# Halved products in the first FFNs of a two-layer hybrid block, and the state space matrices made one third later

## The reference

```python
for l in range(DEPTH):
    x = x + 0.5 * swiglu(rms_norm(x, ffn1_norm[l]), ffn1_w1[l], ffn1_w3[l], ffn1_w2[l])
    h = rms_norm(x, mix_norm[l])
    p = h @ w_in[l]                       # inputs of four branches
    ...                                   # mamba2, s5 (state space), sparse attention, hgrn2
    x = x + merged @ w_out[l]
    x = x + 0.5 * swiglu(rms_norm(x, ffn2_norm[l]), ffn2_w1[l], ffn2_w3[l], ffn2_w2[l])

def swiglu(x, w1, w3, w2):                # w1, w3: 1024 x 2816, w2: 2816 x 1024
    return (jax.nn.silu(x @ w1) * (x @ w3)) @ w2
```

## Time and profile before

| what | value |
|---|---|
| median of 3 runs | 2779.82 us (2779.58 to 2780.38) |
| profiled execution | 2778.9 us, span 2777.1 us |
| granted TensorE clock | 1.00 in the mean |
| TensorE busy | 2771.6 us (100%) |
| its weight loads | 2332.3 us (84%) |
| VectorE, ScalarE, GpSimd busy | 1746.9 (63%), 1272.2 (46%), 845.8 us (30%) |
| DMA | 284.57 MB, mean 102 GB/s |
| chain that ended last | TensorE 98% |

### The profile page before, as it was taken

How to read it: one execution, slowest core, us unless ns; L and a number is a source line. 1 busy time by engine, 2 the same in 40 slices (tenths; PEclk the granted TensorE clock), 3 DMA queues, 4 the chain that set the end, 5 groups by cost and what they waited for, 6 DMA issues and landing times.

```text
span 2777.1 us, 41251 instructions
## 1 busy us (share of the span) xinstructions
PE 2771.6 (100%) x15610; PEld 2332.3 (84%) x15610; DVE 1746.9 (63%) x2736; ACT 1272.2 (46%) x1944; POOL 845.8 (30%) x412
## 2 busy tenths in 40 slices
PE   9999999999999999999999999999999999999999
PEld 8888888877788888898988888888777888898988
DVE  5585557685657447585744855576856674585755
ACT  5343344556355446353543423445553553453533
POOL 0075014333333442131100850233333343421321
PEclk9999999999999999999999999999999999999999
DMA  5323573222222232233333235732222222323323
GB/s 199 98 91 117 142 159 116 82 76 69 81 87 79 90 94 98 91 115 99 107 129 98 91 129 136 159 107 84 69 76 76 84 84 91 94 90 105 108 95 103
DMA packets 113091, 284.57 MB, mean 102 GB/s; under 512 B 35616, under 2 KB 45344, under 8 KB 112416
## 3 DMA queue, kind: packets, MB, share of 16 engines
q1 hardware_dynamic: 112928, 282.35, 32.8%
HBM read 268.67 MB, written 9.44 MB: 100 GB/s over the span
## 4 chain that ended last, share of the span: by engine, by line
PE 98%; DVE 1%; ACT 0%; issue 0%; DMA 0%; SPq 0%; ACTq 0%; DVEq 0%
PE bank L594 25%; PE bank L596 24%; PE bank L595 24%; PE bank L678 5%; PE bank L679 5%; PE bank L680 4%; PE bank L622 1%; PE bank L624 1%; PE bank L623 1%; PE bank L987 1%; PE bank L1006 1%; PE bank L1021 1%; PE bank L767 1%; PE bank L1120 1%; PE bank L961 0%; PE bank L974 0%
## 5 line engine op out<-in xcount | busy, mean ns | idle before, releaser
L464 POOL TENSOR_TENSOR w_lo<-raw,w_hi 128x1024 fp32r<-128x1024 f32 x208 | 519.5, 2502 | 1080.9 <-ACT w_hi L456 1080.9
L594 PE MATMUL bank<-h_hi,w_hi 128*128 128x512 f32 x1872 | 736.8, 394 | 0.6 <-DVE silu_a L2160 0.3
L596 PE MATMUL bank<-h_hi,w_lo 128*128 128x512 f32 x1872 | 729.1, 389 | 0.0
L595 PE MATMUL bank<-h_lo,w_hi 128*128 128x512 f32 x1872 | 728.9, 389 | 0.0
L456 ACT ACTIVATE w_hi<-raw 128x1024 fp32r<-128x1024 f32 x374 | 393.4, 1056 | 562.6 <-PE bank L596 537.4
L594 PEld LDWEIGHTS bank<-h_hi,w_hi 128*128 128x128 f32 x1872 | 351.4, 188 | 80.6 <-issue 7.1
L596 PEld LDWEIGHTS bank<-h_hi,w_lo 128*128 128x128 f32 x1872 | 351.4, 188 | 74.0
L595 PEld LDWEIGHTS bank<-h_lo,w_hi 128*128 128x128 f32 x1872 | 351.6, 188 | 70.7
L464 DVE TENSOR_TENSOR w_lo<-raw,w_hi 128x1024 fp32r<-128x1024 f32 x166 | 230.9, 1391 | 169.7 <-ACT w_hi L456 169.4
L514 POOL TENSOR_TENSOR w_lo<-raw,w_hi 128x1024 fp32r<-128x1024 f32 x76 | 139.3, 1853 | 445.4 <-DVE bank L2211 445.4
L594 PE MATMUL bank<-g_hi,w_hi 128*128 128x512 f32 x698 | 272.1, 390 | 0.2
(11 more groups left out here) (441 smaller groups left out, 5178.3 us busy)
## 6 DMA issues: line engine op xcount, KB each, us to landing
raw<-in_w_lots SPq DMA_DIRECT2D x478, 512.0 KB, 3.5
s_wd<-s_z SPq DMA_DIRECT2D x8, 512.0 KB, 3.5
s_t<-s_taps SPq DMA_DIRECT2D x16, 256.0 KB, 13.2
da_s<-da_qk SPq DMA_DIRECT2D x16, 256.0 KB, 3.9
x<-in_x SPq DMA_DIRECT2D x8, 256.0 KB, 6.0
raw_k<-in_w_lots SPq DMA_DIRECT2D x8, 256.0 KB, 6.3
s_w_re<-s_wd SPq DMA_DIRECT2D x32, 64.0 KB, 3.5
s_w_im<-s_wd SPq DMA_DIRECT2D x32, 64.0 KB, 3.4
```

What stands on the lines that cost most here:

```text
L464: eng.tensor_tensor(w_lo[:, s], raw[:, s], w_hi[:, s].bitcast(f32), SUB).then_inc(S["lo_done"], 1)
L594: pe.matmul(b[:, :], w_hi[:, s, kw], xh[:, k], start=(k == 0), stop=False)
L595: pe.matmul(b[:, :], w_hi[:, s, kw], xl[:, k], start=False, stop=False)
L596: return pe.matmul(b[:, :], w_lo[:, s, kw], xh[:, k], start=False, stop=(k == nk - 1))
```

## The change

- `PLAIN_PAIRS` now has an entry for each FFN of each layer: ffn1 of layer 0 has six plain pairs in its first third, none in the second and six (all) in the last; ffn1 of layer 1 has three, none and six; ffn2 stays as it was. So 2 + 8 = 10 and 5 + 8 = 13 pairs of ffn1 become halved.
- ffn1 uses the code of ffn2 for that (`halved`, `three_plain`), and new code for layer 0 (`six_plain`). ScalarE writes the unrounded h for it (`normed_of`, `hn_first`). The pairs' loops are written out; in the second third the early start of the first two down lots falls away.
- `s5_prepare` moves one third later: phases 0 and 1 at the second third's down lots, 2 behind the last third's pairs, 3 (VectorE) ahead of the last two pairs of the last third, 4 into the last third's down lots, ahead of the last one. TensorE makes the taps behind the sixth of these lots.
- GpSimd first does its share of ffn1's halved pairs, then `s5_matrices`, now with the input matrices (`s5_gen`) ahead of the output ones (`s5_ca_ready`).
- SP: the turned matrices are stored ahead of the third down lot of the last third, 24 of the 32 fetches stand ahead of the lots 64 to 71 (three per lot from lot 64 to 71), the other eight behind the taps' stores, and the lots 72 to 75 behind those.
- In the last tile of the stage before ffn2, `tile_of` makes `h_lo` ahead of the sum of squares.
- Some buffers move.

```diff
-PLAIN_PAIRS = (3, 0, 0)
+PLAIN_PAIRS = (((6, 0, 6), (3, 0, 6)), ((3, 0, 0), (3, 0, 0)))
...
+            def halved(n, i0, J):
+
+                first = n + 2 * i0
+                for a in range(first, n + 2 * J, 2):
+                    q1(a)
+                    if a > first:
+                        q3(a - 2)
+                    q5(a)
+                    q6(a)
+                    if a > first:
+                        q4(a - 2)
+                    q2(a)
+                    q7(a)
+                q3(n + 2 * J - 2)
+                q4(n + 2 * J - 2)
...
+                    if i0 < J:
+                        halved(n, i0, J)
+                    n, g0 = n + 2 * J, g0 + J
+                    if th < len(THIRDS) - 1:
+                        down(n, J, g0)
+                    else:
+                        for j in range(KT):
+                            gemm(n + j, 0, g_hi, g_lo, J, ready=("g_done", g0 - J) if j == 0 else None)
+                            if j == 5:
+                                s5_taps_of()
...
+                for n in range(4, MIX0 + 4):
+                    if n == 12 and layer == 0:
+                        sp.dma_start(con[:, upper:freq], con_in[:, upper:freq]).then_inc(S["c_rest"], 16)
+                    if n == FIRST_LOT[0][1] + 21:
+
+                        sp.wait_ge(S["out_done"], OUT[FIRST_LOT[0][1] + 15] + 1)
...
+                    if n == MIX0 - 6:
+                        for i in range(4):
+                            sp.wait_ge(S["s5_w_turned"], i + 1)
...
+                    if n >= MIX0 - 4:
+                        if n == MIX0 - 4:
+                            sp.wait_ge(S["s5_w_out"], 16 * 4)
+                        fetch_w(3 * (n - MIX0 + 4), 3 * (n - MIX0 + 5))
+                    lot_in(n)
                 sp.wait_ge(S["s5_tap_d"], 4)
                 taps = s5_taps.rearrange("i (j g) c -> g i j c", g=8)
                 for g in range(8):
                     sp.dma_start(taps[g], s5_tap[16 * g:16 * g + 16]).then_inc(S["s5_tap_out"], 16)
-                ring(MIX0 // 4, MIX0 // 4 + 2)
+                fetch_w(24, 32)
+                ring(MIX0 // 4 + 1, MIX0 // 4 + 2)
...
+                    else:
+                        s5_prepare(2)
+                        for j in range(KT):
+                            if j == KT - 1:
+                                s5_prepare(4)
+                            split_hi(act, n + j + 4)
+                            tile_of(1, j, (OUT[n + j], 0))
...
             def tile_of(r, i):
+                if r == 2 and i == KT - 1:
+                    low(r, i)
+                    add_square(r, i)
+                    return
                 add_square(r, i)
                 low(r, i)
...
+                    else:
+                        for j in range(KT):
+                            down(n, j, 0)
+                            split_lo(V, n + j + 4, 0)
+                            tile_of(1, j)
+                            if j == KT - 2:
+                                s5_prepare(4)
```

More of the change, by code:

```diff
@@ L729, in ffn2 @@
                         norm_sums(2)
-                        for j in range(2, 2 * PLAIN_PAIRS[0]):
+                        for j in range(2, 2 * i0):
                             gemm(n + j, 0, h_hi, h_lo, KT)
[L732 to L745, removed]
+                        pe.wait_ge(S["w0_in_t_lo"], s_at(1, S4))
+                    halved(n, i0, J)
                     n, g0 = n + 2 * J, g0 + J
@@ L752, in ffn2 @@
                         return
-                    with pe.Fori(0, 2) as it:
-                        for j in range(4):
-                            gemm(n + j, it, g_hi, g_lo, J, ready=("g_done", g0 - J) if j == 0 else None)
+                    down(n, J, g0)
             def keep_busy(n):
@@ L1297, in _ @@
[L1297 to L1304, removed]
-                sp.wait_ge(S["s5_w_out"], 16 * 4)
@@ L1455, in _ @@
                 OUT.layer = layer
+                halved(0)
                 s5_matrices()
                 mixing()
[L1458 to L1470 removed]
+                halved(1)
         @block.scalar
@@ L1590, in round_g, with round_s, plain @@
                 act.activation(g_hi[:, i], gated[:, i % 2], AFT.Copy).then_inc(S["g_hi_done"], 1)
+            def round_s(which):
+                for j in S_SUMS:
+                    act.wait_ge(S["x7_in_t_sum"], s_at(which, j))
+                    act.activation(s_hi[j][:, :, :], sm[j][:, :, :], AFT.Copy).then_inc(S["x0_in_t_hi"], 1)
+            def plain(n, i, g):
+                split_hi(act, n + 4)
+                silu(n, i % 2, g)
+                split_hi(act, n + 5)
+                round_g(i, g)
@@ new lines, in halved @@
+            def halved(n, i0, J, g0):
+                for i in range(i0, J):
+                    a = n + 2 * i
+                    more = i + 1 < J
+                    high(act, a + 2)
+                    if i0 and i == i0:
+                        copy_x(a)
+                        round_g(i - 1, g0)
+                    else:
+                        if i >= i0 + 2:
+                            round_g(i - 2, g0)
+                        copy_x(a)
+                    if more:
+                        round_weights(a + 2, a)
+                    else:
+                        copy_v(a)
+                        high(act, a + 3)
+                    if i > i0:
+                        silu(a - 2, (i - 1) % 2, g0)
+                round_g(J - 2, g0)
+                high(act, n + 2 * J + 2)
+                high(act, n + 2 * J + 3)
+                silu(n + 2 * J - 2, (J - 1) % 2, g0)
+                round_g(J - 1, g0)
```

652 lines of the change are left out of this document (349 added, 303 removed).

## The result

| | before | after |
|---|---|---|
| median of the runs | 2779.6 us (2779.5 to 2780.4) | 2793.6 us (2788.3 to 2794.4) |
| profiled execution: span, time | 2777.1, 2778.9 us | 2791.8, 2793.6 us |
| mean granted clock | 1.00 | 0.995 |

The kernel became slower: the ratio is 1.0045 with a 95% interval of 1.0033 to 1.0056. The time lies in the forecast's range, 5.6 us above its likeliest value.

The account below looks back on a forecast made before the run. TensorE, busy for 100% of the span, was taken to bound the kernel. Terms -18.8 (halved pairs), -0.5 (h_lo), +23.8 (stalls) and +4.0 (clock) gave +8.5 us: time 2787.4, median about 2788, range 2774 to 2797.

Parts of the forecast that it names:

- Halved pairs: First FFNs of both layers: halving the pairs shortens TensorE's matmuls by 18.8 us in all, with no wait there.
- the rival without a stall: State space step: u's stores are served beside s_t, not behind it, so no stall; 2760.5 us, chance 0.17.
- I cost it at nothing: New VectorE, ScalarE and GpSimd work for the halved pairs: same code as in ffn2, taken as no loss.
- its own cover: GpSimd's matrix chain, one third later: 96.7 us long, TensorE wants its last matrix 111.6 us later; 15 us remain.
- The queue: SyncE behind the late taps: stores, fetches and weight lots precede s_t, issued at 381.7 us, 9.1 us later than before.
- The second part: Four weight lots ahead of s_t must drain, 5.6 us at 375 GB/s, making u 12.9 us late instead of 9.1.
- the chain of u: Round trip of u through memory before the state space step: 12.9 us later in each layer.
- The stalls: TensorE's wait for u at the state space step: 11.5 and 12.3 us in the two layers, 23.8 in all.
- The rival with issue times alone: Lots ahead of s_t cost only issue times: shift 9.1, stalls 16.2 us, 2781 us with the clock; chance 0.12.
- Line rate: s_t's drain: the skill's 512-byte rule gives some 6 us and no wait; the forecast followed the trace's 124 GB/s.
- The clock: State space step behind the stall: clock falls to 1.2 GHz at least in part, 2 us a layer, 4 in all.
- The rival of a further wait: GpSimd's chain exceeds 112 us beside a busier VectorE, or SP brings last down-stage lots late; 2795 to 2805 us, chance 0.08.

## Why the prediction was right, and where not

**Halved pairs.** Forecast 18.8 us, measured 19.0 by the stages. That TensorE never waits in a halved stage held in every run. The run with the taps behind lot 3 and the pause closes the sum: with no wait left but those of the program's first microseconds the time is 2760.6 us, and the rival without a stall had said 2760.5.

**"I cost it at nothing."** For the new work of the halved pairs this was right. The step that failed is its neighbour, the matrices one third later: I gave GpSimd's chain its own length and its own cover (15 us; it measured 16.7 without TensorE's wait) and asked only whether TensorE would wait for the chain. I did not ask what the chain does to VectorE, which in this third has TensorE right behind it: 5.5 us of waits for g_lo and 1.6 of clock. The pause shows this as the cause.

In the traces in which GpSimd works beside the pair only the instructions with both inputs in SBUF are longer; the first, which reads a bank, takes 0.69 us in every one. The Trainium skill ("SBUF — State Buffer", Who interferes with whom) says just this: a VectorE instruction with two SBUF inputs contends with a GpSimd instruction that reads SBUF, and one with at most one does not, outside the two-port modes. The trace agrees, and had I held that rule against the chain's new place the wait could have been forecast.

**The queue.** The order of SyncE's queue was read rightly. In times of the kernel before (TensorE reaches the step at 414.37 there and at 409.34 here, so 5.03 are added), the taps are ready at 370.3 (forecast 370.45), s_t is issued at 382.8 (381.7): 10.2 us late for 9.1, since the eight fetches take 5.1 us in the queue and not 3.8. The second part, 3.8 us more for the drain of the lots, was too large: it measured 1.3 and 3.6, and 2.1 on the mean of the five runs (26.7 against 24.6). One cause is a row that I had not shown. I wrote that before "everything else found the queue empty", but SyncE's timeline of the kernel before has a lot right ahead of s_t:

```profile
355.70 16.65 SPq L1270 DMA_DIRECT2D raw<-in_w_lots  x5
```

The last of these five was issued at 372.0, 0.6 us ahead of s_t. By my own reckoning it is through 0.8 us after s_t's issue at 372.62, and that leaves 3.0 us of the 3.8. The rest differs between layers and runs and was not found.

Together the chain of u was late by 11.5 us in layer 0 and, with s_t 10.5 us late there, 14.1 in layer 1: 25.6 for twice 12.9. That the sum fits is partly luck, since the fetches were longer and the drain shorter than forecast. The stalls are 9.0 and 12.9 us for 11.5 and 12.3, together 21.9 for 23.8, and what is missing lies behind u: the last load of u landed 4.2 us after its issue in layer 0, where I had put the slowest landing of the kernel before (5.3), and u's loads were issued in 11.3 instead of 11.8 us in layer 1. The rival with issue times alone (16.2) is further off, and the rival in which u's stores are served beside s_t is ruled out by the run without s_t.

**Line rate.** The rule of the Trainium skill on the smallest transfer for line rate ("DMA: Bandwidth & Descriptors", Specifications) would have given no wait. The trace disagrees: in 383 to 400 us the packets, 3810 of 4032 between 512 bytes and 2 KB, moved at 127 GB/s with the engines full. This does not show that the size of the packets sets the rate. Each load of s_t also writes only 16 partitions (`s5_t[16 * i:16 * i + 16]`), where a weight lot writes 128, and no run changes one and keeps the other.

**The clock.** Forecast 2 us in each layer, measured 2.0 and 2.3; the run with 48 matmuls in the wait shows it for what it is. In the other runs that kept the whole wait (lots first, transposes earlier, pause) the step lost between 1.2 and 2.2 us behind 8.8 to 11.8 us of waiting, so its size too is met only roughly. Here the sign of the Trainium skill's rule ("TensorE: Matmul & The Clock Gate", HAM oscillation), a cold start behind a wait for a DMA, is confirmed by the windows at 0.62, 0.74 and 0.50.

**The sum.** +8.5 forecast, +14.2 found: 5.5 + 1.6 for g_lo, 0.4 more for the clock, 0.3 at the start, against 1.9 less of stall and 0.2 more gain. The rival of a further wait (2795 to 2805) had the right kind of loss, GpSimd's chain beside VectorE, but put it at TensorE's wait for the chain. The time fell in the range by luck: the range reached 9 us above the forecast for cases other than the one that filled it.

**What stays open.** The runs of the kernel after lie at 2788 to 2790 or near 2794. The kernels whose s_u wait is gone spread by 2.3 to 5 us too, the paused one with that wait by 6. The wait's length differed between layers and runs by 4 us, which could make such groups; only profiled executions show it, so this was not shown. Nor was it found what sets the rate at which s_t drains.

## What to carry to other kernels

When work is moved to another stage, ask three things of its new neighbours: who waits behind its last result in each queue, whether its engine slows an engine that is just ahead of the critical one, and what else the queue's waiting instruction holds up. Here the arithmetic saved (19 us) was real, and the kernel was 14 us slower with it, or 12.5 us faster once the small product of the taps stood three lots earlier, or 19 us faster with GpSimd's pause as well (and the taps two lots earlier). A short pause on an engine with slack, while an engine just ahead of the critical one does its last piece, gave back 7.5 us in the two last down stages. It cost nothing as long as the slack lasted: with the taps behind lot 2 the paused chain made TensorE wait for 1.5 us in all.

## What the runs showed of the hardware that was not expected

- A wait of TensorE of 2.65 to 3.0 us can already be followed by the lower level of the clock (1.2 of 2.4 GHz): six to eight matmuls of 512 columns then start 0.43 us apart in place of 0.23, and 1.5 to 1.7 us are lost. In the kernel after it happened in layer 1 (window at 0.52) and not in layer 0, whose wait was 0.2 us longer; in the run with the early taps it was the reverse. In the seven runs with this wait it happened 11 times out of 14, so its length alone does not decide it.
- VectorE beside GpSimd, in the last pair: 0.69 became 1.53 to 1.80 us for 128x512 with two SBUF inputs, and 1.22 became 2.19 for 128x1024; 0.69 stayed 0.69 with one input from a bank.
- The loads of s_t drained at 104 to 106 GB/s in layer 1 of the kernel after and at 105 to 132 in layer 0, behind the same four lots, which themselves moved at 376; with one lot ahead it was 99 to 102 in the run with the lots first. All 16 DMA engines were busy either way (a share of 1.24 to 1.28), so a full share says little about the rate.
